# Expert sweeps of the two PEER layers: the up product of a row tile as three 256-column matmuls into one half bank instead of a 512- and a 256-column matmul whose two halves VectorE adds

## The reference, cut to what matters

```
g = jax.nn.softmax(top_s, axis=-1)
ue = jnp.take(u_tab, ids, axis=0)
ve = jnp.take(v_tab, ids, axis=0)
act = jax.nn.gelu(jnp.einsum("nd,nhkd->nhk", hb, ue).astype(jnp.float32))
return jnp.einsum("nhk,nhkd->nd", (g * act).astype(hb.dtype), ve)
```

## Time and profile before

| | |
|---|---|
| median of 3 runs | 4116.48 us (4115.08 to 4119.59) |
| span of the profiled execution, first to last instruction | 4127.8 us |
| the profiled execution's own time beside its span | none was recorded; the span stands for it |
| TensorE busy (matmuls) | 3958.7 us, 96% of the span |
| TensorE weight loads busy | 3263.7 us, 79% |
| VectorE busy | 2825.2 us, 68% |
| ScalarE busy | 1573.8 us, 38% |
| granted TensorE clock, mean | 0.976 of 2.4 GHz |

### The profile page before, as it was taken

One profiled execution on the slowest core, in us unless ns is written; L12 is line 12 of the kernel. 1 busy time (PEld: TensorE's weight loads), 2 busy tenths in 40 slices (PEclk: granted clock), 3 DMA queues, 4 the chain that ended last, 5 costly groups with the idle time before them and its releaser, 6 DMA issues.

```text
span 4127.8 us, 62206 instructions
## 1 busy us (share of the span) xinstructions
PE 3958.7 (96%) x21266; PEld 3263.7 (79%) x21266; DVE 2825.2 (68%) x5134; ACT 1573.8 (38%) x2444; POOL 83.3 (2%) x92
## 2 busy tenths in 40 slices
PE   7899899799989999999999999999978999999998
PEld 7797789445867888888888888888747888888887
DVE  6342265795798777777698777777471897777776
ACT  5201052231147444444218444444322165444443
POOL 0000000000000000000000000000310000000000
PEclk9899999999999999999999999999969999999999
DMA  5213355575544666666652666666664625666664
GB/s 186 69 50 102 102 180 162 171 236 170 171 152 136 188 189 188 188 189 188 203 155 78 196 188 188 188 188 201 167 218 137 189 88 163 188 188 189 188 190 144
DMA packets 209895, 686.41 MB, mean 166 GB/s; under 512 B 36544, under 2 KB 46800, under 8 KB 208736
## 3 DMA queue, kind: packets, MB, share of 16 engines
q1 hardware_dynamic: 173728, 627.88, 48.5%
q0 software_dynamic: 11712, 47.29, 3.8%
q10 hardware_dynamic: 24320, 9.37, 0.9%
HBM read 659.36 MB, written 24.05 MB: 166 GB/s over the span
## 4 chain that ended last, share of the span: by engine, by line
PE 91%; DVE 6%; DMA 1%; ACT 1%; issue 1%; SPq 0%; DVEq 0%; ACTq 0%
PE psum L1017 26%; PE psum L1003 16%; PE psum L1005 8%; PE psum L1082 7%; PE psum L591 6%; PE psum L1118 4%; PE psum L645 4%; PE psum L669 4%; PE psum L1214 3%; PE psum L890 1%; PE psum L982 1%; PE psum L1283 1%; PE psum L1067 1%; DMA ring<-in_w 1%; PE psum L1294 1%
## 5 line engine op out<-in xcount | busy, mean ns | idle before, releaser
L1017 PE MATMUL psum<-rows_split_odd,coef_split 128*128 128x512 f32 x2400 | 589.4, 395 | 2.1 <-DVE rows_split_odd L2245 1.1
L2250 DVE TENSOR_REDUCE work<-psum 128x256 f32<-128x512 f32 x356 | 246.3, 692 | 502.3 <-PE psum L1005 502.3
L1017 PE MATMUL psum<-rows_split,coef_split 128*128 128x512 f32 x2208 | 532.2, 390 | 0.3 <-issue 0.3
L1017 PEld LDWEIGHTS psum<-rows_split_odd,coef_split 128*128 128x128 f32 x2400 | 436.7, 188 | 104.1 <-issue 4.8
L1003 PE MATMUL psum<-input_split,rows_split 128*128 128x512 f32 x1424 | 508.2, 397 | 1.2 <-ACT arena L1370 1.2
L1003 PE MATMUL psum<-input_split,rows_split_odd 128*128 128x512 f32 x1424 | 504.3, 393 | 0.0
L1563 ACT ACTIVATE work<-work 128x256 f32<-128x256 f32 x356 | 149.0, 419 | 855.7 <-DVE work L2250 855.7
L1017 PEld LDWEIGHTS psum<-rows_split,coef_split 128*128 128x128 f32 x2208 | 402.1, 188 | 81.7 <-issue 0.9
L2245 DVE TENSOR_TENSOR rows_split_odd<-ring,rows_split_odd 128x1024 fp32r<-128x1024 f32 x378 | 460.1, 1218 | 6.4 <-ACT rows_split_odd L1370 6.4
L1370 ACT ACTIVATE rows_split_odd<-ring 128x1024 fp32r<-128x1024 f32 x378 | 398.5, 1055 | 163.7 <-PE psum L1017 161.0
L2245 DVE TENSOR_TENSOR rows_split<-ring,rows_split 128x1024 fp32r<-128x1024 f32 x362 | 440.5, 1217 | 4.5 <-ACT rows_split L1370 4.4
(11 more groups left out here) (414 smaller groups left out, 5094.2 us busy)
## 6 DMA issues: line engine op xcount, KB each, us to landing
ring<-in_w SPq DMA_DIRECT2D x420, 512.0 KB, 3.6
ring<-in_u SPq DMA_DIRECT2D x384, 512.0 KB, 3.6
ring<-in_v SPq DMA_DIRECT2D x384, 512.0 KB, 3.5
scratch_inj<-stage ACTq DMA_DIRECT2D x16, 512.0 KB, 5.5
arena<-scratch_inj POOLq DMA_DIRECT2D x7, 1024.0 KB, 7.9
scratch_cm<-work POOLq DMA_DIRECT2D x8, 512.0 KB, 5.2
scratch_cm<-arena POOLq DMA_DIRECT2D x8, 512.0 KB, 6.3
arena<-scratch_parked POOLq DMA_DIRECT2D x4, 1024.0 KB, 8.8
```

The source lines that it names most:

```text
L1017: last = mm(bank(2 + 2 * i + f), CFR[:, b, c, P * i:P * i + P], parts[:, v, 512 * f:512 * f + 512], start=(first and c == 0 and v == 0), s ...
L2250: dve.tensor_reduce(AC[:, b, :], bank(b).rearrange("p (x t) -> p t x", x=2), AX, ALU.add)\
```

## The change

`up` makes three matmuls of 256 columns for each k, all into the low half of bank b, so that the bank holds the finished sum. `total` and its semaphore `sum_ready` go. `gelu` waits for `up_ready`, reads the half bank in PSUM, writes `AC`, and so waits also until the coefficients of tile j-2 have been made out of the same half of `AC`. up(j+2) waits for `gelu_done` of tile j. VectorE's list is now low v(j), coef(j), low u(j+2). Of the diff, the calls of `total` that are dropped in the opening, the loop and the end of VectorE's list are shown once.

```diff
                     if not first:
-                        pe.wait_ge(sem("sum_ready"), j + (s0 - e - 1))
+                        pe.wait_ge(sem("gelu_done"), j + (n0 - 1))
                     pe.wait_ge(sem("u_low"), j + (s0 - e + 1))
                     for k in range(8):
-                        mm(bank(b), SPL[b][:, 0, 0, P * k:P * k + P], HR[:, k, :, :], start=(k == 0), stop=False,
-                           skip_group_check=True)
-                        last = mm(bank(b)[:, 0:S], SPL[b][:, 0, 1, P * k:P * k + P], HR[:, k, 0, :], start=False,
-                                  stop=(k == 7), skip_group_check=True)
+                        for u, x in ((0, 0), (0, 1), (1, 0)):
+                            last = mm(bank(b)[:, 0:S], SPL[b][:, 0, u, P * k:P * k + P], HR[:, k, x, :],
+                                      start=(k == 0 and u == 0 and x == 0), stop=(k == 7 and u == 1),
+                                      skip_group_check=True)
                     last.then_inc(sem("up_ready"), 1)
...
-                def gelu(j, b):
-                    act.wait_ge(sem("sum_ready"), j + (STEADY[p] - e + 1))
-                    f(AC[:, b, :], AC[:, b, :], ACT.Gelu_apprx_tanh).then_inc(sem("gelu_done"), 1)
+                def gelu(j, b, first=False):
+                    act.wait_ge(sem("up_ready"), j + (n0 + 1))
+                    if not first:
+                        act.wait_ge(sem("coef_ready"), j + (n0 - 1))
+                    f(AC[:, b, :], bank(b)[:, 0:S], ACT.Gelu_apprx_tanh).then_inc(sem("gelu_done"), 1)
...
                 for b in range(2):
-                    gelu(e + b, b)
+                    gelu(e + b, b, not e)
...
-                def total(j, b):
-                    dve.wait_ge(sem("up_ready"), j + (n0 + 1))
-                    dve.tensor_reduce(AC[:, b, :], bank(b).rearrange("p (x t) -> p t x", x=2), AX, ALU.add)\
-                        .then_inc(sem("sum_ready"), 1)
-
...
                 for i in L.loop((NEXP - 2 - e) // 2 - 1, 4):
                     for b in range(2):
-                        total(i * 2 + (e + b + 2), b)
                         low(1, i * 2 + (e + b + 2), b, w0 + 2 * e + 6 + 2 * b)
                         coef(i * 2 + (e + b + 2), b)
                         low(0, i * 2 + (e + b + 4), b, w0 + 2 * e + 7 + 2 * b)
```

More of the change, by code:

```diff
@@ L2273, in split_experts @@
                 for b in range(2):
-                    total(e + b, b)
                     low(1, e + b, b, w0 + 2 * e + 2 + 2 * b)
@@ L2284, in split_experts @@
                 for b in range(2):
-                    total(NEXP - 2 + b, b)
                     low(1, NEXP - 2 + b, b, w0 + 2 * NEXP - 2 + b)
```

## The result

| | before | changed |
|---|---|---|
| runs with the prediction, median | 4117.23 us (4 runs) | 4148.98 us (4 runs) |
| ratio, 95% interval | | 1.0075 (1.0061 to 1.0089) |
| later, on one chip in turn (e5), median | 4124.12 us (15 runs) | 4144.36 us (11 runs) |
| ratio, 95% interval | | 1.0050 (1.0034 to 1.0065) |
| span of the profiled execution | 4127.8 us | 4149.5 us |

The change made the kernel slower, by 0.75% in the first comparison and 0.50% in the second. 4143 us was forecast, 4121 to 4158 as a range. One further run of the kernel before, in the slow state at 18,661 us, is left out of the second comparison.

A forecast was written before the change was run, and what follows sets the result against it. TensorE's matmul stream was taken to bound the sweeps. Extra matmuls +28.5 us and ends -1.9 us gave +26.6 us, so the runs' median of 4116.5 us became 4143 us (+0.65%), range 4121 to 4158.

The forecast's parts named there:

- TensorE's stream alone sets the sweeps' time, and VectorE's sum is worth nothing in the steady tile: Steady sweeps: TensorE always busy; dropping 246.3 us of VectorE reductions, nearly all in 2.4 us of slack per tile, saves nothing.
- The ends and the first start, -1.9 us: Three sweep ends and first sweep's start: TensorE no longer waits about 0.47 us at each, -1.9 us in all.
- Gelu out of PSUM: ScalarE's 356 Gelu activations read the bank: 0.47 us each taken, against 419 ns before, and nothing for the time.
- The waits and SyncE's queue: up(j+2) waiting for gelu(j) has 7.6 us of slack; SyncE's fills wait no longer than before: 0.
- the rival of gaps in the loop: TensorE's loop, now 72 matmuls a turn: one 0.3 us gap in each of 175 turns, +52 us, 4196 us; chance 0.05.
- The extra matmuls, +28.5 us: Up products: three matmuls at 0.120 us, 0.360 for 0.350 us a step, +0.08 us a tile over 356 tiles.
- the signs that I had named for being wrong: Profile after: up-product starts at 0.117 us or less, changed down products, TensorE idle per turn or before up, sweep clock not 1.00.
- The fixed cost of 0.010 us a matmul: TensorE's sweep matmuls: time is columns plus 0.010 us, fitted to 0.230 (down), 0.120 (L645) and 0.350 us (up pair).
- The weight load is the floor: Rival for up products: the load sets 0.116 us a matmul, three make 0.349; 4111.6 us, no change; chance 0.05.
- The small fixed time of 0.0026 us: Rival: each of 2848 extra matmuls costs 0.0026 us, +7.4 less 1.9; 4122 us, no measurable change; chance 0.07.
- the faster case: Rival: the 512-column form is slow, 256 columns take 0.108 us; -74 less 1.9, 4040.5 us; chance 0.05.

The follow-up runs named there:

- e5: The changed kernel unedited, timed again on one chip in turn with the kernel before: 4144.36 us, ratio 1.0050.
- e3: Changed kernel with the two matmuls of before in `up`; sum left out, Gelu reads the bank's low half: 4115.74 us, ratio 0.9981.
- e10: As e9, with VectorE taking low v ahead of the sum in all sweeps: 4117.54 us, ratio 0.9976.
- e2: Kernel before with only the matmuls changed to three of 256 columns per k, VectorE's sum and old waits kept: 4140.37 us, ratio 1.0039.
- e4: Changed kernel with the third matmul of each step cut into two of 128 columns, a weight load each: 4432.68 us, ratio 1.0741.
- e12: Changed kernel with six matmuls of 128 columns per step instead of three of 256, each with its weight load: span 5029.8 us.
- e6: Changed kernel with weight loads of 64 columns instead of 128 in the up product: up 2.73 us (rows_split) and 2.84 (rows_split_odd), tile 5.57.
- e11: Changed kernel with the buffer edit of e9: up 2.80 us, down 2.755, tile 5.553 in sweeps 2 and 3.
- e8: Changed kernel with the two row buffers exchanged in the third sweep alone: there up 2.87 us with rows_split, 2.80 with rows_split_odd.
- e9: Kernel before with, in sweeps 2 and 3, all up rows in rows_split_odd and all down rows in rows_split: 4108.75 us, ratio 0.9957.

## Why the prediction was right, and where its reasons were not

- **TensorE's stream alone sets the sweeps' time, and VectorE's sum is worth nothing in the steady tile**: shown by e3, where 246 us of VectorE's work are gone and the tile stays at 5.56 us.
- **The ends and the first start, -1.9 us**: -2.4 us in e3, 2.0 us in e10, by the path described (coefficients before the down product is due): the last down product starts 2.73 us after the one before it in e3, and started 3.20 us after it before.
- **Gelu out of PSUM**: harmless as said, but the price was guessed on the wrong side: 385 ns a time against 419 ns out of SBUF before, not 470.
- **The waits and SyncE's queue**: no idle of TensorE before any steady product; the rival of gaps in the loop didn't come.
- **The extra matmuls, +28.5 us**: the right sign, and mis-sized: 21.1 us (e2), 0.06 us a tile for 0.08. The term fares worse than these numbers look. The up products, all that it counted, grew by 0.06 and 0.015 us, 0.039 on average, which is 14 us over 356 tiles and half of the forecast. The other 7 us are in the down products, which were to stay at 2.73 and 2.79 us. The 0.120 us read from L645 is right for the up products out of `rows_split` (2.87 / 24 = 0.120) and wrong for those out of `rows_split_odd` (2.805 / 24 = 0.117). So two of the signs that I had named for being wrong came true (starts at 0.117 us, a changed down product), in a forecast whose total held.
- **The fixed cost of 0.010 us a matmul**, which I took because three rows agreed on it, is refuted below 256 columns by e4 and e12. Columns + 0.010 would give a 128-column matmul 0.065 us; in a stream it takes 0.111. Two free numbers had been fitted to three rows, and rows of 256 and 512 columns could not show the bend below them. What the runs show in its place: a stream in which each matmul has a full weight load goes at about 0.11 us a matmul, whether 128 or 64 columns pass (e12), most likely because of the load. 256 columns need 256 / 2.4 = 0.107 us at the granted clock of 1.00, about the same pace, while a 512-column matmul at 0.23 is far above it. That 256-column matmuls take 0.117 to 0.120 us because columns and load are about equally long there is my reading, and it is not shown: narrow loads sped them up with one buffer and slowed them with the other (e6).
- **The rivals.** "The weight load is the floor" named a real limit at the wrong price. Its 0.116 us was (2.02 - 0.28) / 15 over a group whose first two starts lie 0.185 us apart; the others of that group lie 0.111 to 0.112 apart. Its sum has a slip too: 3 x 0.116 is 0.348 us, so it should have forecast -5.7 us instead of -3, and 4109 us. It forecast no change, and the kernel got slower. The small fixed time of 0.0026 us and the faster case are out: no up product of 256-column matmuls with full loads came below 0.1166 us a matmul (2.798 / 24, e11). With it falls, for this stream, the Trainium skill's rule of N / 2.4 + about 2.5 ns ("TensorE: Matmul & The Clock Gate", section "Wait — 56ns, not 53.3ns?"), whose estimated 0.109 us for 256 columns no such run reached. The gaps in TensorE's loop did not come.
- **The forecast of the time** held partly by luck: a term twice too large in the up products, a cost in the down products that it did not have, and the rest of the span. 26.6 us were expected, the sweeps show 19.0, and the medians of the two comparisons lie 31.8 and 20.2 us apart.

**What stays open.** Why the buffer counts. e8, e9 and e11 show that it does and that it goes with the buffer, not with the tile. By the kernel's allocations `rows_split` lies directly below `input_split` in SBUF, and `coef_split` a little below `rows_split_odd` with only a small tensor between, and the products that pair these neighbours are the slower ones (2.81 for 2.79 and 2.79 for 2.73 in the kernel before); that the nearness is the cause was not tried, since it needs other places for the token parts. Also open are the 0.04 us that the down product out of `rows_split` takes more when the up products beside it are of three matmuls (e2 shows it isn't the other engines' order). By its single starts this is no cost of the change from one product to the other: before, the matmuls follow each other after 0.227 us from the second on; in the changed kernel only the last three of the twelve do, and those before them after 0.231 us on average. Open, too, are why 256-column matmuls take 0.117 to 0.120 us, more than either their columns or the load asks, and the 0.005 us by which narrow loads slowed `rows_split_odd` in e6. Nothing was measured of what moves the granted clock in the part from 2950 to 3190 us.

## What to carry to other kernels

Count weight loads as well as columns: where every matmul has a 128 x 128 load of its own, a matmul of 128 columns takes 0.111 us and one of 256 takes 0.117 to 0.120, so a matmul of 256 columns cut in two costs nearly twice the time. An engine that is the bound should not be given more and narrower matmuls to spare an engine that has slack. Change the buffers before the instructions if products of one shape differ by their buffer. Before a cost per instruction is carried from one stage to another, fit it on a third width, well away from the two that it was made from. When a stage repeats to 0.2 us and the whole kernel only to some 20, judge the edit by the stage's own marks in the trace, and keep the timed runs for the sign.

## What the runs showed of the hardware that was not expected

- In a stream, matmuls that each have a 128 x 128 weight load follow each other after about 0.11 us, with 128 moving columns (e12, 0.111) and with 64 (L1283, 0.112), at a granted clock of 1.00; with loads over 64 rows 64 columns follow after 0.062 us (L1261).
- The same product on the same shapes costs about 2% more or less with the SBUF buffer that holds its rows: 2.87 or 2.81 us (three-matmul up), 2.73 or 2.79 (down, kernel before). Giving each role the buffer that suits it made tiles 5.51 us for 5.56 and the sweeps 11 us shorter (e9; 0.29% to 0.58% in the timed runs).
- A product's time depends on the form of the product beside it: the down product out of `rows_split` took 2.73 us beside up products of 16 matmuls, 2.77 beside 24 (e2), 2.80 beside 32 (e4) and 2.82 beside 48 (e12). In e4 and e12 about 0.05 us of it stand before its second matmul (0.28 for 0.235 us), so they may belong to the up product ahead.
- ScalarE's Gelu over 256 columns took 385 ns out of PSUM and 419 ns out of SBUF.
